# Router logits as partial sums in four column groups of TensorE, and the expert biases' rounded copies on ScalarE, in a one-core decoder layer

## The reference

```python
x = x + mixed @ w_out
h = rms_norm(x, g_ffn)
logits = (hf @ w_router + b_router).astype(jnp.float32)
top_v, top_i = lax.top_k(logits, TOP_K)
gates = jax.nn.softmax(top_v, axis=-1)
...
u = xb @ w_e1[e] + b_e1[e]
x_glu = jnp.minimum(u[..., ::2], SWIGLU_LIMIT)
x_lin = jnp.clip(u[..., 1::2], -SWIGLU_LIMIT, SWIGLU_LIMIT)
act = x_glu * jax.nn.sigmoid(SWIGLU_ALPHA * x_glu) * (x_lin + 1.0)
return act @ w_e2[e] + b_e2[e]
```

## Time and profile before

| | |
|---|---|
| Median of 3 runs | 1182.59 us (1182.31 to 1187.12) |
| The profiled execution's own time | 1183.14 us |
| Its span, first to last instruction | 1180.3 us, so 2.84 us lie around it |
| Busy in the span | TensorE 1134.0 us (96%), VectorE 420.7, ScalarE 255.9, GpSimd 139.5 |
| Moved | 447.67 MB, 379 GB/s over the span |
| GB/s in 40 slices of 29.5 us | 297 229 156 197 143 130 242 300 337 416, then 425 to 436 in every slice but the last |

### The profile page before, as it was taken

The page is one execution under the profiler, slowest core; times in us unless marked ns, Lnnn a source line. Parts: engine busy times, 40 slices in busy tenths (PEclk is TensorE's granted clock), DMA queues, the critical chain, the costliest instruction groups (busy, mean ns, idle before and its releaser), DMA issues.

```text
span 1180.3 us, 17838 instructions
## 1 busy us (share of the span) xinstructions
PE 1134.0 (96%) x7335; PEld 551.0 (47%) x7335; DVE 420.7 (36%) x817; ACT 255.9 (22%) x441; POOL 139.5 (12%) x98
## 2 busy tenths in 40 slices
PE   7999999999999999999999999999999999999996
PEld 5988999985333333333333333333333333333331
DVE  6888743855222222222222222222222222222223
ACT  5465846342111111111111111111111111111112
POOL 5445553561000000000000000000000000000000
PEclk9999999999999999999999999999999999999999
DMA  7645336789999999999999999999999999999995
GB/s 297 229 156 197 143 130 242 300 337 416 428 428 427 426 429 431 431 432 433 431 433 432 429 436 430 431 433 430 434 429 434 432 430 435 431 425 428 429 426 244
DMA packets 28386, 447.67 MB, mean 379 GB/s; under 512 B 3312, under 2 KB 3696, under 8 KB 5920
## 3 DMA queue, kind: packets, MB, share of 16 engines
q1 hardware_dynamic: 27920, 446.77, 90.1%
q10 hardware_dynamic: 432, 0.42, 0.1%
HBM read 446.12 MB, written 1.05 MB: 379 GB/s over the span
## 4 chain that ended last, share of the span: by engine, by line
PE 66%; DMA 25%; DVE 7%; issue 1%; SPq 1%; ACT 1%; DVEq 0%; another core or an unknown queue 0%
PE PS L907 38%; DMA EXT<-wexp 24%; PE PS L634 12%; PE PS L900 4%; PE PS L892 3%; PE PS L924 2%; PE PS L683 1%; PE PS L759 1%; DVE ROW L1766 1%; DVE ROW L1769 1%; DVE BRW L1762 1%; DVE slot_R L1315 1%; PE PS L733 1%; DVE EXT L1353 1%; DMA EXT<-be 1%
## 5 line engine op out<-in xcount | busy, mean ns | idle before, releaser
L907 PE MATMUL PS<-ring,MX 128*64 128x512 f32 x1536 | 349.8, 597 | 14.6 <-DMA ring<-wexp 13.8
L907 PEld LDWEIGHTS PS<-ring,MX 128*64 128x64 f32 x1536 | 103.5, 136 | 226.0 <-issue 194.8
L1262 ACT ACTIVATE TAB<-BRW 128x256 f32<-128x256 f32 x64 | 26.7, 417 | 592.9 <-DVE BRW L1762 592.9
L566 POOL TENSOR_TENSOR slot_R<-ring,slot_R 128x512 fp32r<-128x512 f32 (+1 forms) x76 | 118.2, 1586 | 107.5 <-ACT slot_R L1062 107.5
L907 PE MATMUL PS<-EXT,TAB 128*64 128x512 f32 x512 | 120.1, 600 | 3.4 <-DMA EXT<-wexp 3.4
L907 PE MATMUL PS<-ring,TAB 128*64 128x512 f32 x512 | 119.9, 600 | 3.4 <-DMA ring<-wexp 3.4
L907 PE MATMUL PS<-EXT,MX 128*64 128x512 f32 x512 | 116.9, 598 | 0.9 <-DMA EXT<-wexp 0.2
L1762 DVE TENSOR_SCALAR BRW<-PS 128x256 f32<-128x256 f32 x64 | 27.2, 425 | 241.8 <-PE PS L907 241.8
L634 PE MATMUL PS<-slot_R 128*128 128x256 f32 (+2 forms) x288 | 90.1, 313 | 0.0
L1062 ACT ACTIVATE slot_R<-ring 128x2048 fp32r<-128x2048 f32 (+1 forms) x38 | 70.8, 1868 | 39.0 <-DMA ring<-wblk 21.6
L900 PE MATMUL PS<-MX,BRW 64*128 64x512 f32 x264 | 74.2, 640 | 0.8 <-DVE MX L1781 0.8
(11 more groups left out here) (262 smaller groups left out, 1154.9 us busy)
## 6 DMA issues: line engine op xcount, KB each, us to landing
ring<-wexp SPq DMA_DIRECT2D x40, 4096.0 KB, 45.1
ring<-wexp SPq DMA_DIRECT2D x44, 2048.0 KB, 19.5
EXT<-wexp SPq DMA_DIRECT2D x20, 4096.0 KB, 46.7
EXT<-wexp SPq DMA_DIRECT2D x21, 2048.0 KB, 17.6
ring<-wblk SPq DMA_DIRECT2D x36, 1024.0 KB, 4.8
ring<-wexp SPq DMA_DIRECT2D x8, 1024.0 KB, 9.5
EXT<-wexp SPq DMA_DIRECT2D x6, 1024.0 KB, 42.9
BRW<-brow SPq DMA_DIRECT2D x7, 256.0 KB, 5.5
```

The lines of the kernel that those rows point to most:

```text
L566: last = nc.gpsimd.tensor_tensor(w_unit(u, True)[:, part], w_unit(u)[:, part], h_unit(u, True)[:, part].bitcast(F32), ALU.subtract)
L907: last = mm(PS[g * SLOTS:(g + 1) * SLOTS, b, :], lhsT, rhs[:, g * 512:(g + 1) * 512], start=start, stop=stop)
L1262: fn(SGM[h], GLU, ACT.Sigmoid, scale=ALPHA).then_inc(sgm_ready, 1)
```

## The change

Five edits. (1) The remainder of unit 1 is made by VectorE and that of unit 3 by GpSimd, instead of the other way round. (2) ScalarE makes both rounded copies of each bias part (`bias_high`), between its roundings of weight units; VectorE only subtracts (`bias_rest`). A part may be copied when the subtraction before it is done. (3) VectorE's order changes with it: the remainder of unit 34 and the second subtractions stand ahead of the evacuation of half 30. (4) The logits are made as partial sums: TensorE's four column groups take four of the eight k each, VectorE copies the result (LGP), and a second product with a one-hot table adds the four groups. (5) Small moves in the router: the mean of squares is made behind the scaling, the square root takes its bias from a column, the remainders of the scale and the negated maxima are made later, and the first expert's bias matmuls no longer wait for its scaled tokens; SyncE's chunk C_HT goes out behind the partial logits.

```diff
@@ by_pool
-            return u % 2 == 1 and u != 3 or u == 18
+            return u % 2 == 1 and u != 1 or u == 18
@@ sync
-            sp.wait_ge(lg_full, 1)
+            sp.wait_ge(lgp_full, 1)
             first_chunk(C_HT)
@@ tensor
+            def part_logits(n):
+
+                for g in range(4):
+                    k = 4 * n + g
+                    pe.wait_ge(xnT_ready, k // 2 + 1)
+                    last = mm(PS[g * NE:(g + 1) * NE, 4, 0:SEQ], WR[:, k, :], xnT[:, k, :], start=(n == 0), stop=(n == 1),
+                              skip_group_check=True)
+                return last
+
+            def logits():
+
+                pe.wait_ge(lgp_ready, 1)
+                for i in range(TT):
+                    last = mm(PS[:, 5, i * NE:(i + 1) * NE], LGP[:, i * P:(i + 1) * P], TAB[:, T_HOT:T_HOT + NE],
+                              start=True, stop=True)
                 return last
...
             new_x_t(1, [0])
+            part_logits(0)
+            new_x_t(1, [1])
             residual(0, 0)
-            new_x_t(1, [1])
-            logits(0)
-            logits(1).then_inc(lg_full, 1)
+            part_logits(1).then_inc(lgp_full, 1)
+            logits().then_inc(lg_full, 1)
...
-                pe.wait_ge(xt_ready, e + 1)
+                if not (turn is FIRST and j == 0):
+                    pe.wait_ge(xt_ready, e + 1)
                 for h in range(2):
                     both_halves(4 + h, SELE, BE1[:, h * D:(h + 1) * D], True, False)
+                if turn is FIRST and j == 0:
+                    pe.wait_ge(xt_ready, 1)
@@ scalar
-            for u in range(29, NU - 3):
-                split(u)
+            def bias_high(part, dst, raw, base, done):
+
+                if part:
+                    act.wait_ge(done, 2 * part)
+                else:
+                    act.wait_ge(be_in, 32)
+                places = [dst[(base + n) % 3 * NE:((base + n) % 3 + 1) * NE] for n in range(3)]
+                if part < 2:
+                    fn(places[2 - part], raw, ACT.Copy)
+                fn(places[0], raw, ACT.Copy).then_inc(done, 1)
+
+            def biases_high(part):
+
+                bias_high(part, BE1, BE1R, 0, be1_ready)
+                bias_high(part, BE2, BE2R, 1, be2_ready)
+
+            split(29)
+            split(30)
+            biases_high(0)
+            split(31)
+            split(32)
+            biases_high(1)
+            split(33)
+            split(34)
+            biases_high(2)
@@ vector
+            rest(1)
             rest(2)
-            rest(3)
...
+            def bias_rest(part, dst, raw, base, done):
+
+                hi = dst[base % 3 * NE:(base % 3 + 1) * NE]
+                dve.wait_ge(done, 2 * part + 1)
+                v.tensor_tensor(raw, raw, hi, ALU.subtract).then_inc(done, 1)
...
-            biases1(0)
             rest(30)
...
                 if i == 13:
-                    biases2(0)
                     rest(32)
+                    biases_rest(0)
                 else:
-                    biases1(1)
-                    biases2(1)
+                    rest(34)
+                    biases_rest(1)
...
                 if i == 15:
-                    rest(34)
-                    biases1(2)
-                    biases2(2)
                     rest(36)
...
+            dve.wait_ge(lgp_full, 1)
+            v.tensor_copy(LGP, PS[:, 4, 0:SEQ]).then_inc(lgp_ready, 1)
```

More of the change, by code:

```diff
@@ L88 @@
 C_GMIX, C_BQ, C_BK, C_BGA, C_BGB, C_BGATE, C_GFFN, C_BLR = 0, 8, 12, 16, 24, 32, 36, 44
-NCV = 45
+C_EPS = 45
+NCV = 46
 R_SINK, R_HEAD, R_ROUTER = 0, 16, 272
@@ L909, in both_halves @@
                 return last
-            pe.wait_ge(rsp_in, 1)
             pe.wait_ge(sel_ready, 1)
@@ L1241, in _ @@
                 square(q)
+                act.wait_ge(ssq1, q + 1)
+                high(q)
                 if q < 3:
-                    act.wait_ge(ssq1, q + 1)
-                    high(q)
                     middle(q)
             act.wait_ge(var1, 1)
-            fn(S_SD, S_VAR, ACT.Sqrt).then_inc(sd1, 1)
-            act.wait_ge(ssq1, 2 * TT)
-            high(2 * TT - 1)
+            fn(S_SD, S_SS, ACT.Sqrt, scale=1.0 / D, bias=col(C_EPS)).then_inc(sd1, 1)
             middle(2 * TT - 1)
@@ L1341, in _, with biases_rest @@
                                         HT_R[:, 2 * n:2 * n + 2, :].bitcast(F32), ALU.subtract).then_inc(ht_ready, 1)
+            rest(1)
             rest(2)
-            rest(3)
[L1345 to L1363, removed]
+            def bias_rest(part, dst, raw, base, done):
+                hi = dst[base % 3 * NE:(base % 3 + 1) * NE]
+                dve.wait_ge(done, 2 * part + 1)
+                v.tensor_tensor(raw, raw, hi, ALU.subtract).then_inc(done, 1)
+            def biases_rest(part):
+                bias_rest(part, BE1, BE1R, 0, be1_ready)
+                bias_rest(part, BE2, BE2R, 1, be2_ready)
             def token_major(u, dst, w, done=None):
@@ L1668, in _ @@
             link(v.tensor_tensor(left, rs, S_RP[:, :, 0:1], ALU.subtract))
-            link(v.tensor_copy(S_RP[:, :, 1:2], left))
-            v.tensor_tensor(S_RP[:, :, 2:3], left, S_RP[:, :, 1:2], ALU.subtract).then_inc(rsp_in, 1)
             dve.wait_ge(lg_full, 1)
             for i in range(TT):
-                last = v.scalar_tensor_tensor(LG[:, i, :], PS[:, 4 + i, 0:NE], S_RS[:, i:i + 1],
+                last = v.scalar_tensor_tensor(LG[:, i, :], PS[:, 5, i * NE:(i + 1) * NE], S_RS[:, i:i + 1],
                                               ROW[:, R_ROUTER:R_ROUTER + NE], ALU.mult, ALU.add)
@@ L1689, in _ @@
             v.tensor_reduce(MK, OH.rearrange("p i k e -> p i e k"), AX_X, ALU.max).then_inc(mask_ready, 1)
-            for i in range(TT):
-                v.tensor_scalar(S_NV[i], S_V8[i][:, 0:1], -1.0, None, ALU.mult).then_inc(top_ready, 1)
             dve.wait_ge(mask_ready, 1)
-            link(v.tensor_scalar(BIG, MK, -1e6, 1e6, ALU.mult, ALU.add))
+            v.tensor_scalar(BIG, MK, -1e6, 1e6, ALU.mult, ALU.add)
+            link(v.tensor_copy(S_RP[:, :, 1:2], left))
+            link(v.tensor_tensor(S_RP[:, :, 2:3], left, S_RP[:, :, 1:2], ALU.subtract))
             dve.wait_ge(rank_full, 1)
@@ L1712, in _ @@
             v.tensor_tensor(SEL, iota, spread(RK[:, :, 0:1]), ALU.is_equal).then_inc(sel_ready, 1)
+            for i in range(TT):
+                v.tensor_scalar(S_NV[i], S_V8[i][:, 0:1], -1.0, None, ALU.mult).then_inc(top_ready, 1)
             v.tensor_copy(SELE, hot(slice(T_HOT, T_HOT + 1))).then_inc(sele_ready, 1)
```

23 lines of the change are left out of this document (12 added, 11 removed).

## The result

The median of 17 runs is **1190.25 us** (1187.5 to 1191.31), beside 1183.59 us for the kernel before on the same chips: ratio 1.0046, 95% interval 1.0034 to 1.0058. The ratio is of the fast executions alone, since one of the kernel before took 6478 us. The kernel is slower by 4.0 to 6.9 us, and whether that is over the 0.5% of the prediction the interval doesn't tell. The profiled execution took 1190.13 us, with a span of 1188.2 (before 1183.14 and 1180.3).

The account below looks back on a forecast made before the run. TensorE was taken to limit the kernel to about 245 us (block 16's end), then the unbroken weight stream. Terms -0.5 - 0.76 + 2.3 + 5.9 = +6.9 us took the profiled 1183.14 to 1190.0, median forecast 1189.5 us, range 1183 to 1193.

Parts of the forecast that it names:

- First new wait: Block 15's second half: TensorE waits 2.3 us for VectorE's evacuation of half 28, behind remainder and bias subtractions.
- the branch "1.1 us shorter": If VectorE is served before GpSimd at 217.3 us, each new wait's chain is up to 1.1 us shorter: 1188.4 us.
- Second new wait: Block 16's second half: TensorE waits 5.9 us for VectorE's evacuation of half 30, reckoned to end at 243.6 us.
- Rival 1: TensorE's clock falls to 1.2 GHz in the long wait, costing none or 2.6 us: 1191 to 1192 us; chance 0.20.
- Rival 2: VectorE and GpSimd don't alternate on the 32-row subtractions, only slow one another a little: 1184.3 us; chance 0.16.
- Rival 3: Evacuations are in time, so neither new wait is left and the old waits are gone: 1181.3 us; chance 0.16.
- Half 26: Near 212 us: TensorE's old wait for VectorE's evacuation of half 26 goes, -0.76 us.
- Exchange: Units 1 and 3 change engines: TensorE's early waits for remainders shrink, bounds 0 to 0.9 us gained, taken as -0.5 us.
- Router 0: Behind 245 us: the router's edits save TensorE some 1.5 us, counted as 0 because queued transfers hide it.
- 4.4 us of cover: Transfers queued ahead of the chunk issued behind the logits, said also to hide logits costing 2 us more.
- The sum: -0.5 - 0.76 + 2.3 + 5.9 = +6.9 us at the end of block 16, all of it reaching the kernel's end.

Follow-up runs that it names:

- Experiment 4: Changed kernel with 20 and 34 unneeded matmuls of 256 columns added ahead of the two waiting halves: 1187.27 us, ratio 1.0037 to the kernel before.
- experiment 3: Changed kernel with each round of bias subtractions put ahead of the remainder of unit 32 or 34 on VectorE: 1180.38 us, ratio 0.9971 to the kernel before.
- 1: Changed kernel with the biases split as before, back on VectorE; unit exchange and router edits stay: 1181.41 us, ratio 0.9973 to the kernel before.
- 5: Kernel before with the router's edits alone: 1182.55 us, ratio 1.0001.
- 7: Kernel before with 25 unneeded matmuls of 256 columns (3.0 us) in block 15: 1185.51 us, ratio 1.0029.
- 8: Kernel before with 14 unneeded matmuls of 512 columns (3.0 us) ahead of the first gather: 1186.11 us, ratio 1.0030.
- 10: Kernel before with 7 unneeded matmuls of 512 columns (1.5 us) ahead of the first gather: 1184.52 us, ratio 1.0008.
- 12: Kernel before with the exchange of units 1 and 3 between VectorE and GpSimd alone: 1184.00 us, ratio 0.9996.
- experiment 11: Changed kernel with the bias subtractions ahead of the remainders and the router of the kernel before: 1179.99 us, ratio 0.9966 to the kernel before.
- 6: Kernel before with the biases' change alone (ScalarE's copies, VectorE's subtractions and new order): 1189.29 us, ratio 1.0069.
- 2: Changed kernel with the exchange of units 1 and 3 undone: 1189.33 us, ratio 1.0051 to the kernel before.

## Why the prediction was right, and where only in sum

- **First new wait, +2.3:** measured 2.66. VectorE was served first (the branch "1.1 us shorter"), but GpSimd began 1.6 us later than I took (216.38 for 214.80, since unit 31's data were there at 214.39 and not at 212.80), so BE2, which I had reckoned free, met its last quarter: 2.18 us for 1.22. The evacuation began at 226.66 us, reckoned 225.5; TensorE came for it at 224.7, reckoned 223.9.
- **Second new wait, +5.9:** 2.79 stood still. The step's frame, the end of that wait, was right: reckoned 243.6 less 0.5, measured 243.41. That it fits to 0.3 us is in part luck: the grid stood 1.3 us later at 216 us than reckoned, and the branch in which VectorE is served first took 1.1 off. TensorE came to the wait 2.9 us later than reckoned (240.6 for 237.7), 1.7 of it by the slow clock, and so stood 3.1 us less. What ends this wait doesn't hang on when TensorE comes: in the rows above ScalarE's copies start when VectorE's first subtraction is over (224.45), the two units are rounded without a pause behind them, and VectorE goes on when the second is rounded (234.20). So a slow stretch ahead of such a wait costs nothing.
- **Rival 1, the clock:** this is the step that was mis-sized. I gave it 0.20 and looked at the long wait alone; it fell at both waits, of 2.66 and 2.79 us, and elsewhere after 1.75. "The other waits are far shorter" was no argument against it: the one row I had, 2.5 to 7.5 us of standstill, bounds the fall from above only. Its price at the end was 1.7 us, that of the second stretch, where I had set none or 2.6. Experiment 4 has 2.1 from the profiles and 3.0 from the medians, and what makes the rest was not separated. The rule of the Trainium skill that I set beside it (TensorE: Matmul & The Clock Gate, section "Why this matters for your kernels") pointed the right way where my row didn't; but the falls came at waits shorter than the gaps it warns of, and there the measurement decides.
- **Rival 2, no alternation:** out, by 3.38, 2.18 and 9.16 us in the rows above. The Trainium skill (SBUF — State Buffer, section "SBUF: two separate sides") agrees with them.
- **Rival 3:** out for this order. It is what experiment 3 reaches, by the order and not by cheaper copies: 1180.4 us where I had reckoned 1181.3.
- **Half 26, -0.76:** the wait is gone. By other executions it was worth more: 1.2 to 2.1 us in the profiles of 1, 5, 7, 8, 10 and 12, since it starts at a transfer's landing.
- **Exchange, -0.5:** the two waits are gone from the trace; the times of the runs don't show the gain, but the traces do. Where the clock rises early, the grid's point at 203 to 204 us is at 202.96 to 203.59 in the five profiles with the exchange and at 203.73 to 203.82 in the four without, on average 0.55 us apart; where it rises late, 204.61 and 204.72 stand against 204.76 to 204.91, 0.16 apart.
- **Router 0, with 4.4 us of cover:** the 0 holds by medians (experiments 5 and 11). The cover does not: 3 us more cost 3.5 (experiment 8). The 4.4 us were transfers queued ahead of C_HT, but what must not come late is the first ring place at 282 us, which I didn't look at. The old router is just about level with the transfers there, the changed kernel 1.9 us ahead. Over all profiles the lead-in is 67.6 to 68.6 us while the first ring place is issued 35.6 to 37.7 us behind the first chunk (69.1 at 37.5 in the kernel before), and 69.2 to 72.3 at 38.3 to 41.2. So if the four groups had not overlapped and the logits had cost 2 us more, most of that would have been paid (an estimate from experiments 8 and 10: 3.5 us for 3.0 and 1.2 for 1.5).
- **The sum:** the first chunk was forecast at 251.8 us and went out at 253.83: 0.3 by the end of the second wait, 1.7 by the slow stretch behind it. The 1.3 us won back behind it and the 0.9 less around the span, neither of which I had, took 2.2 us off again: the execution took 1190.13 us where 1190.0 was reckoned. So the ends of the waits were sized right, and beyond them the total was right because misses cancel.

What stays open: why the clock falls in the old router in some executions and not in others, what makes the start's rise vary, and whether the four column groups or the small moves make the router's 1.3 us; these were not separated.

## What to carry to other kernels

When small work moves into an engine's program, ask first on what the instruction ahead of it waits: the same subtractions cost 0.8% behind a remainder that was not ready, and nothing in the idle time ahead of it. Price a standstill of TensorE of two or three microseconds as the standstill and, in addition, a possible slow stretch at its end, and then ask whether another wait swallows that stretch. For cover, look for the first transfer that the shortened or lengthened work itself releases, not for the transfers that happen to be queued.

## What the runs showed of the hardware

- The granted clock fell to 0.50 in, or within 1.6 us behind, waits of TensorE of 1.75 (1), 2.66, 2.79 (changed) and 4.22 us (6), for 3.4 us each time, and for 6.8 us at one of 3.48 (2). Waits of 0.50 (before), 1.17 (10), 1.28 (8), 1.47 (5), 1.90 (2), 1.91 (7), 2.09 (6) and 2.11 us (12) had no fall near them. So the length of a wait of about 2 us does not decide it alone.
- It fell without any wait while the old logits of 32 columns ran (experiment 11), but not in every execution.
- At the start the same eight matmuls took 2.08 or 3.75 us by execution. Between profiles with an early and a late rise the grid differs by 1.4 us on average with the exchange and by 1.0 without, as much as the smaller edits of this change bring.
- Matmuls with 32 output columns in four column groups started within 0.02 us of one another, four at a time (changed kernel, 276.85 us).
- VectorE's subtraction of 32 x 2048 took 2.28 us with GpSimd idle (3, 211.03 us) and 3.38 beside it, that of 32 x 1024 1.22 and 2.18.
- The biases' transfer was used at 205.66 us in one execution and at 206.60 in another whose grid was 0.7 us earlier, so a wait that hangs on it varies by over 1 us.
